# A mixer of attention and state-space heads in rounds of two jobs and two heads, with the weights' difference added while turned

## What is computed

```python
# attention branch: 8 heads, two score maps each, one subtracted from the other
a = probs(q1b, k1) - lam * probs(q2b, k2)
o = einsum('bhqk,bhkv->bhqv', a, v)            # then an RMS norm over each head's 64 columns
# state-space branch: 16 heads of 64 columns, in two groups of 8
y = einsum over keys of (C B^T * decay) with x*dt   # written over the whole 256 x 256 causal map
y = (y + xs * d_skip) * silu(z)                # then an RMS norm over each group's 512 columns
mixed = concatenate([attn, ssm]) @ w_out
```

## Times and the profile before

| | us |
|---|---|
| timed runs | 1287.53, 1287.18, 3872.66 (median 1287.53) |
| the profiled execution | 1286.62 |
| its span, first to last instruction | 1284.8 |
| mean granted clock of TensorE | 0.982 |

### The profile page before, as it was taken

How to read it: one execution, slowest core, us unless ns; L and a number is a source line. 1 busy time by engine, 2 the same in 40 slices (tenths; PEclk the granted TensorE clock), 3 DMA queues, 4 the chain that set the end, 5 groups by cost and what they waited for, 6 DMA issues and landing times.

```text
span 1284.8 us, 19110 instructions
## 1 busy us (share of the span) xinstructions
PE 1223.2 (95%) x7700; PEld 1058.4 (82%) x7700; DVE 839.2 (65%) x1308; ACT 656.0 (51%) x1076; POOL 230.9 (18%) x284
## 2 busy tenths in 40 slices
PE   7897899999999889999999999999999889999996
PEld 6785588888888568888888889999996579888996
DVE  6955586665586467666657776467766756766743
ACT  6425566644333556664446555446635444655531
POOL 4003431110000332121112221000005201112101
PEclk9999999999999999999999999999999879999999
DMA  7790155564454324555544554543440024455461
GB/s 275 269 200 14 54 197 171 190 222 174 163 197 155 141 99 173 188 196 194 184 182 162 196 198 153 197 175 141 162 185 1 1 77 162 164 196 175 155 206 56
DMA packets 34088, 205.56 MB, mean 160 GB/s; under 512 B 3776, under 2 KB 6352, under 8 KB 13776
## 3 DMA queue, kind: packets, MB, share of 16 engines
q1 hardware_dynamic: 30704, 200.47, 44.0%
q10 hardware_dynamic: 3296, 3.87, 1.6%
HBM read 202.87 MB, written 1.46 MB: 159 GB/s over the span
## 4 chain that ended last, share of the span: by engine, by line
PE 79%; DVE 14%; ACT 3%; POOL 1%; issue 1%; DMA 0%; POOLq 0%; ACTq 0%; DVEq 0%
PE ps L660 35%; PE ps L665 23%; PE ps L663 5%; PE ps L664 5%; DVE wl L602 4%; PE ps L684 1%; PE ps L686 1%; PE ps L685 1%; DVE tf L2173 1%; POOL pb L992 1%; PE ps L907 1%; PE ps L973 1%; ACT wh L573 1%; DVE y L1960 1%; DVE xb L738 1%
## 5 line engine op out<-in xcount | busy, mean ns | idle before, releaser
L602 DVE TENSOR_TENSOR wl<-raw,wh 128x2048 fp32r<-128x2048 f32 (+4 forms) x196 | 421.2, 2154 | 150.6 <-ACT wh L573 150.4
L660 PE MATMUL ps<-xb,wh 128*128 128x512 f32 x1424 | 502.3, 398 | 4.4 <-DVE wl L602 3.9
L665 PE MATMUL ps<-xb,wl 128*128 128x256 f32 x1696 | 476.2, 281 | 0.0
L573 ACT ACTIVATE wh<-raw 128x2048 fp32r<-128x2048 f32 (+4 forms) x196 | 348.6, 1781 | 157.9 <-PE ps L665 123.6
L660 PEld LDWEIGHTS ps<-xb,wh 128*128 128x128 f32 x1424 | 267.4, 188 | 71.1 <-issue 5.6
L665 PEld LDWEIGHTS ps<-xb,wl 128*128 128x128 f32 x1696 | 321.5, 190 | 0.0
L665 PE MATMUL ps<-ab,wl 128*128 128x256 f32 x1088 | 307.2, 282 | 0.0
L660 PE MATMUL ps<-ab,wh 128*128 128x512 f32 x640 | 226.8, 399 | 0.8 <-DVE ab L1002 0.8
L665 PEld LDWEIGHTS ps<-ab,wl 128*128 128x128 f32 x1088 | 207.0, 190 | 0.0
L660 PEld LDWEIGHTS ps<-ab,wh 128*128 128x128 f32 x640 | 120.2, 188 | 31.7 <-DVE ab L1002 1.4
L857 DVE TENSOR_TENSOR tf<-ps,tf 128x256 f32<-128x256 f32 x148 | 61.9, 421 | 119.3 <-ACT tf L852 119.3
(11 more groups left out here) (326 smaller groups left out, 1372.1 us busy)
## 6 DMA issues: line engine op xcount, KB each, us to landing
raw<-wstream SPq DMA_DIRECT2D x156, 1024.0 KB, 4.8
raw<-wstream SPq DMA_DIRECT2D x32, 704.0 KB, 4.1
raw<-wstream SPq DMA_DIRECT2D x8, 768.0 KB, 4.2
e_bt<-scratch ACTq DMA_DIRECT2D x16, 128.0 KB, 9.7
o_bt<-scratch SPq DMA_DIRECT2D x2, 1024.0 KB, 10.2
raw<-wstream SPq DMA_DIRECT2D x2, 560.0 KB, 10.1
raw<-wstream SPq DMA_DIRECT2D x4, 256.0 KB, 6.4
h<-xt ACTq DMA_DIRECT2D x4, 256.0 KB, 7.5
```

Of the source, the lines that this page charges most:

```text
L573: e.g.activation(WH[i % HLN][:, 0:w], RAW[i % RAWN][:, 0:w], ACT.Copy).then_inc(S["hi"], 1)
L602: e.g.tensor_tensor(WL[q][:, 0:w], RAW[i % RAWN][:, 0:w], f32(WH[q][:, 0:w]), ALU.subtract).then_inc(S["lo"], 1)
L660: e.g.matmul(PS[b][:, :].rearrange("p (a t) -> p a t", a=2), wh[:, sl], x2[:, :, cs], start=start, stop=k == p.nk - 1, skip_group_check=pair)
L665: ins = e.g.matmul(o, wl[:, sl], xh[:, cs], start=False, stop=k == p.nk - 1, skip_group_check=pair)
```

## The change

The mixer's loop goes from 30 steps to 13 rounds, and a round takes one attention head (two jobs) and two state-space heads. The map of decays is laid out so that its first two blocks have one bias.
- **PE.** `pe_decay(p)` builds heads 2p and 2p+1 in banks 3 and 4. The fp32 product for the first block is gone; the split of dt*a into two fp32r parts (SPL, now for both token blocks) is multiplied with two 256-column stretches of trir: four fp32r products of 256 columns and two masks. `pe_states(p)` does the products of the two heads interleaved, `pe_mixer_scores(h)` the scores of the head's two jobs interleaved (banks 7 and 2), `pe_mixer_pv(s)` the value products of two heads interleaved. `pe_mixer_turn(h)` does six accumulating products with the identity as the moving operand, for each block the first job's weights and then the second's, instead of three transposes of a sum. A round is: group sum, scores(i), turn(i-1), decay(i+2), states(i+1), in odd rounds a value pair, attention sum.
- **ACT.** Two exponentials for a state-space head, not three. Its round is: exponentials of two jobs, copy of turn(i-1), `act_decay(i+2)`, m_oa in odd rounds, late steps.
- **POOL.** Weights one of the two state-space heads (`weighted`), squares for the attention norm, multiplies y by silu(z), squares and sums it, and weighs both jobs (`pool_weigh`).
- **DVE.** Maxima of two jobs, weights the other state-space head, adds d_skip*x, late steps, then both reciprocals, the second times -lambda.
- **Before the loop.** Decays 0 and 1 and the xt and cb products stand ahead of mv, states(0) behind it. m_eb has four buffers; m_xdt and m_eb lie elsewhere, so some of the ah copies wait for the last state product. `MIXK` puts state-space tiles first.
- **The even attention.** ACT takes jobs 2 and 3's exponentials before ev1's outputs; DVE computes the gates of one token block in step 7 and of the other in step 9; the compressed branch's transposes move from step 6 to step 11.

The core of the diff:

```diff
-MIXK = [0, 1, 2, 4, 5, 6, 7, 8, 9, 10, 11, 3]
+MIXK = [4, 5, 0, 6, 7, 1, 8, 9, 2, 10, 11, 3]
...
+        def pe_mixer_turn(e, h):
+            A = MIX
+            j = A.pv_base + h
+            b = A.TB[0]
+            e.wait_ge(S["wt"], A.base + 2 * h + 2)
...
+            for x in range(3):
+                s = slice(x * 128, x * 128 + 128)
+                e.g.matmul(PS[b][:, s], PB[2 * h % 4][:, s], c_("ident"), start=True, stop=False)
+                ins = e.g.matmul(PS[b][:, s], PB[(2 * h + 1) % 4][:, s], c_("ident"), start=False, stop=True)
+            ins.then_inc(S["tp"], 1)
...
# pe_mixer
+            pe_decay(e, 1)
+            pe_toks(e, G["mv"], x_ready(5))
+            pe_states(e, 0)
+            for i in range(ROUNDS):
+                for kind, s, step in late_steps(i):
+                    if (kind, step) == ("grp", 1):
+                        e.wait_ge(S["gq"], 4 * s + 4)
+                        pe_sums(e, "ones512", (ACC, ACC2)[s][:, :], nb_no(kind, s))
+                if i < 8:
+                    pe_mixer_scores(e, i)
+                if 0 <= i - 1 < 8:
+                    pe_mixer_turn(e, i - 1)
+                if i + 2 < 8:
+                    pe_decay(e, i + 2)
+                if i + 1 < 8:
+                    pe_states(e, i + 1)
+                if i % 2 and 0 <= i - 3 < 8:
+                    pe_mixer_pv(e, (i - 3) // 2)
+                for kind, s, step in late_steps(i):
+                    if (kind, step) == ("sub", 2):
+                        e.wait_ge(S["sbq"], s + 1)
+                        pe_sums(e, "head64", TMP[0][:, 0:T], nb_no(kind, s))
...
# pool_mixer
+            for i in range(ROUNDS):
+                if i + 1 < 8:
+                    weighted(i + 1)
                 for kind, s, step in late_steps(i):
                     if kind == "sub" and step == 1:
                         e.wait_ge(S["oa"], s + 1)
...
+                if i < 8:
+                    acc, y = (ACC, ACC2)[i // 4][:, :], Y[:, tile(i)]
+                    e.wait_ge(S["yd"], i + 1)
+                    e.wait_ge(S["zs"], 4)
+                    e.link(e.g.tensor_tensor(y, y, m_zs[:, tile(i)], ALU.mult))
...
+                    for j in (2 * i, 2 * i + 1):
+                        pool_weigh(e, A, j, A.base + j)
...
# dve_mixer
+            for i in range(ROUNDS):
+                for j in (2 * i, 2 * i + 1):
+                    if j < A.n:
+                        dve_max(e, A, j)
+                if i + 1 < 8:
+                    weighted(i + 1)
+                if i < 8:
+                    y = Y[:, tile(i)]
+                    e.wait_ge(S["sy"], i + 1)
...
                 for kind, s, step in late_steps(i):
...
+                for j in (2 * i, 2 * i + 1):
+                    if j < A.n:
+                        e.wait_ge(S["ex"], A.base + j + 1)
+                        r = rs(j)
+                        if j % 2 == 0:
+                            e.g.reciprocal(r, sm(j)).then_inc(S["iv"], 1)
...
         def late_steps(i):
-            return ([("sub", s, i - 4 * s - 6) for s in range(4) if 1 <= i - 4 * s - 6 <= 4]
-                    + [("grp", g, i - 7 * g - 7) for g in range(2) if 1 <= i - 7 * g - 7 <= 6])
+            return ([("grp", g, i - 4 * g - 3) for g in range(2) if 1 <= i - 4 * g - 3 <= 4]
+                    + [("sub", s, i - 2 * s - 2) for s in range(4) if 1 <= i - 2 * s - 2 <= 4])
...
# the even attention
                 if i == 2:
+                    act_exp_biased(e, A, 2)
+                    act_exp_biased(e, A, 3)
                     act_gemm(e, G["ev1"], drain=act_toks(G["ev1"], e_v, 512, 0), ahead=0)
...
-                if i == 4:
-                    dve_even_gates(e)
+                if i in (7, 9):
+                    dve_even_gates(e, i // 9)
```

More of the change, by code:

```diff
@@ new lines, in pe_decay @@
+        def pe_decay(e, p):
+            e.wait_ge(S["spl"], 1)
+            for x in range(2):
+                h, ps = 2 * p + x, PS[DB[x]]
+                if p == 0:
+                    e.wait(G["mixer"].free.get(DB[x]))
+                else:
+                    e.wait_ge(S["sx"], h - 2 + 1)
+                for part in range(2):
+                    e.g.matmul(ps[:, 0:256], SPL[:, 32 * part + h:32 * part + h + 1].broadcast_to([128, 128]),
+                               trir[:, 128:384], start=part == 0, stop=False, skip_group_check=True)
+                for part in range(2):
+                    a = 32 * part + 16 + h
+                    e.g.matmul(ps[:, 128:384], SPL[:, a:a + 1].broadcast_to([128, 128]), trir[:, 0:256], start=False,
+                               stop=False, skip_group_check=True)
+                e.g.matmul(ps[:, 0:128], identb[:, :], maskkb[:, :], start=False, stop=False, skip_group_check=True)
+                e.g.matmul(ps[:, 256:384], identb[:, :], maskkb[:, :], start=False, stop=True,
+                           skip_group_check=True).then_inc(S["sd"], 1)
@@ new lines, in pe_states @@
+        def pe_states(e, p):
+            if p == 0:
+                e.wait(G["mixer"].free.get(YB))
+                e.wait(G["xt3"].out[0])
+            else:
+                e.wait_ge(S["yd"], p)
+            e.wait_ge(S["smu"], p + 1)
+            e.wait_ge(S["smv"], p + 1)
+            o = [PS[YB][64 * x:64 * x + 64, :] for x in range(2)]
+            vs = [slice(64 * (2 * p + x), 64 * (2 * p + x) + 64) for x in range(2)]
+            for x in range(2):
+                e.g.matmul(o[x][:, 0:256], m_xdt[0][:, vs[x]], eb(p, x)[:, 0:256], start=True, stop=False)
+            for x in range(2):
+                ins = e.g.matmul(o[x][:, 128:256], m_xdt[1][:, vs[x]], eb(p, x)[:, 256:384], start=False, stop=True)
+            ins.then_inc(S["sy"], 1)
@@ L2418, in pe_mixer_scores @@
+        def pe_mixer_scores(e, h):
+            A = MIX
+            ps = [PS[b] for b in A.SB]
+            t0, sl = (h // 2) * T, slopeb[:, h * 128:h * 128 + 128]
+            p_ = [slice(64 * (h % 2) + 32 * x, 64 * (h % 2) + 32 * x + 32) for x in range(2)]
+            if h == 0:
+                e.wait(G["mixer"].free.get(2))
+                e.wait_ge(S["na"], 1)
                 e.wait(G["mk"].out[1])
             else:
-                e.wait_ge(S["ex"], A.base + i - 2 + 1)
-            e.g.matmul(ps[:, 0:128], m_q[p_, t0:t0 + 128], m_k[p_, t0:t0 + 128], start=True, stop=False)
@@ new lines, in pe_mixer_turn @@
+        def pe_mixer_turn(e, h):
+            A = MIX
+            j = A.pv_base + h
+            b = A.TB[0]
+            e.wait_ge(S["wt"], A.base + 2 * h + 2)
+            if h:
+                e.wait(turned(j - 1))
+            else:
+                e.wait(G["mixer"].free.get(b))
+            for x in range(3):
[3 more added lines that the diff above has]
+            ins.then_inc(S["tp"], 1)
@@ new lines, in pe_mixer_pv @@
+        def pe_mixer_pv(e, s):
+            A = MIX
+            if s == 0:
+                e.wait(G["mixer"].free.get(OB))
+                e.wait(G["mv"].out[1])
+            else:
+                e.wait_ge(S["oa"], s)
+            hs = (2 * s, 2 * s + 1)
+            for h in hs:
+                e.wait(turned(A.pv_base + h))
+            for h in hs:
+                e.g.matmul(PS[OB][64 * (h % 2):64 * (h % 2) + 64, 0:256], m_v[0][:, 64 * h:64 * h + 64],
+                           PT[(A.pv_base + h) % 3][:, 0:256], start=True, stop=False)
+            for h in hs:
+                e.g.matmul(PS[OB][64 * (h % 2):64 * (h % 2) + 64, 128:256], m_v[1][:, 64 * h:64 * h + 64],
+                           PT[(A.pv_base + h) % 3][:, 256:384], start=False, stop=True).then_inc(S["pv"], 1)
```

373 lines of the change are left out of this document (144 added, 229 removed).

## The result

The kernel after takes 1283.2 us in the median of 7 runs (1278.65 to 1284.39), the kernel before 1287.85 in the same comparison: a ratio of 0.9952, 95% interval 0.9933 to 0.997. A second comparison, of 12 runs against 21, gave 0.9961 (0.9945 to 0.9977). So the change makes the kernel 0.4 to 0.5% faster, 5 us, where 1290, 2.5 us slower, was forecast. The time lies inside the forecast range, but the forecast had the wrong sign.

The account below looks back on a forecast made before the run. TensorE, busy 95% of the span, was taken as the bound, with other engines binding in parts of the mixer. 1284.8 + 4.6 (mixer) - 2.0 (first attention) = 1287.4 span, 1290.1 median; forecast 1284 to 1296, eight in ten 1278 to 1301.

Parts of the forecast that it names:

- The order of the waits: Mixer loop: in-order POOL and VectorE queues idle TensorE, 3.5 us before scores(4), 4.2 before turn 5.
- The tail: Mixer's end: ScalarE's roots and VectorE's norms free mo's first bank 8.5 us after turn 7.
- the walk's length at full clock: Mixer loop followed wait by wait at full clock: mo starts at 1039.8, against 1040.2 before.
- the entry: Loop's start: decay 0 waits 0.6 us for VectorE's split; loop begins at 967.4, scores(0) end at 969.0.
- the weighing ends 6.7 after its scores: Rounds 0 to 3: 1.2 for maxima, 0.54, 0.5, POOL's 2.3 and 2.05, and waits, before the turn.
- The clock term: Mixer: TensorE work at 1.2 GHz after idle costs 5 us, bounds 0 and 8.3; mo starts at 1044.8.
- First attention: Exponentials of jobs 2 and 3 run under ev1's product; turn 3 comes 2.5 earlier; gain 2.0 us, bounds 0 and 4.5.
- The step from span to median: Whole kernel: the timed runs' median lies 2.7 us above the profiled span, taking 1287.4 to 1290.1.
- The waits overlap more: Rival, mixer: a third of the 26 us idle doesn't come, mo starts at 1036, time 1281; chance 0.24.
- VectorE and POOL keep each other out: Rival, mixer: VectorE operations slowed beside POOL's, 0.3 us lost on each, mo 10 later, time 1300; chance 0.20.
- The turning stays cheap: Rival, mixer turns: an identity product costs as a transpose, 8 us of work go, time 1286; chance 0.03.
- 8 us of saved TensorE work turn into idle time: Mixer loop: TensorE's work falls from 58 to 50 us, but waits leave mo at 1039.8 against 1040.2.

Follow-up runs that it names:

- fill: Kernel after plus 118 small products, results never read, in TensorE's five idle places of the mixer; 1274.6 us, ratio 0.9878.
- turn_half: Kernel after without the second product of each pair in a turn, so the second job's weights are not added; 1280.5 us, ratio 0.992.
- dve_weighted: Kernel after with POOL's product of decays and C.B given to VectorE, which then does both of a round; 1282.7 us, ratio 0.996.
- mixer_only: Kernel after with the first attention's edits taken back, leaving the new mixer; 1289.2 us, ratio 0.9997.
- best3: Kernel after with POOL's square behind the weighings, VectorE's reciprocals ahead of its late steps, and the last sum's bank read earlier; 1267.9 us, ratio 0.983.

## Why the prediction was wrong
**The order of the waits was right.** Idle ahead of round 4's sum, released by POOL's sum: forecast 3.5, measured 3.38. Ahead of turn 5, by POOL's weighing: 4.2 and 4.61. The 5 walked between value pair 2 and turn 7 came as 3.47 ahead of the sum of round 8 and 1.20 ahead of turn 7; which place the 3 stood for the walk does not say. The experiments show the cause that was named: with the square moved the stalls ahead of both group sums vanish. The tail from the last turn's end to mo, 8.5 forecast, was 7.8.

**The failed step is the walk's length at full clock, in "The order".** It put mo at 1039.8, 92.0 us into the mixer (947.82 is its start before), and said "if the clock holds at 1.00 in the loop, mo starts near 1040". `fill` holds the clock, and mo starts 86.0 us in. Against the forecast's milestones (us into the mixer):

| | forecast, full clock | fill | after |
|---|---|---|---|
| scores(0) end | 21.2 | 20.2 | 20.2 |
| turn 0 starts | 27.9 | 25.6 | 25.6 |
| turn 2 starts | 40.0 | 36.9 | 37.0 |
| value pair 0 ends | 44.6 | 41.2 | 41.3 |
| turn 4 starts | 58.0 | 53.2 | 56.2 |
| turn 5 starts | 68.4 | 63.8 | 66.8 |
| turn 6 starts | 74.2 | 69.1 | 74.4 |
| turn 7 ends | 83.5 | 78.2 | 85.1 |
| mo starts | 92.0 | 86.0 | 92.9 |

1.0 us goes at the entry and 2.4 more by the end of value pair 0. The term there was "the weighing ends 6.7 after its scores": turn 0 starts 5.4 after them. POOL in round 0 of the kernel after shows both parts of the 1.3:
```profile
966.36 0.73 POOL L2152 TENSOR_TENSOR y<-y,m_zs 128x256 f32<-128x256 f32 x1 [14.21 <-DVE y L2260]
...
967.17 0.61 POOL L2155 TENSOR_TENSOR acc<-y 128x256 f32<-128x256 f32 x1
...
967.76 1.63 POOL L965 TENSOR_SCALAR pb<-pb,rs 128x128 f32<-128x128 f32 x4
```
A weighing takes 1.63 and not 2.05, and the first head of a group has nothing to add its square to, so that 1.4 us stand ahead of the weighing where 2.3 were walked. In the later rounds the shorter weighing stays. This loop, not TensorE's work, sets rounds 0 to 3 (`turn_half`). Decays at 0.65 for 0.83 and score pairs at 1.42 for 1.6 add up to 16x0.18 + 8x0.18 = 4.3 us less work, less 0.4 for the state pairs, but only part of it is on the path. Another 1.7 us go by the end of value pair 1 (62.6 against 57.5), 1.3 of them between scores(4) and turn 4, walked at 7.8 and measured at 6.5 in `fill`; 0.9 go behind it.

**The clock term was under, not over.** 5 us were taken of 0 to 8.3; the new mixer pays 6.9. The two errors, -6.0 and +1.9, give 92.9 in place of 97.0: the mixer is 0.5 us longer than in the profile of before, not 4.6.

**What the clock term was held against was missed altogether.** The sum went against one execution of the kernel before, whose mixer had 27 us of low clock, and whose clock of 0.982 is above the kernel's mean of 0.979. Other executions have 34 and 41. The new rounds always have 27. So the mixer part is neutral against the execution that was read, and the median of before was not that execution's.

**First attention.** The mechanism was right (the exponentials of jobs 2 and 3 run under ev1, turn 3 comes 2.9 earlier by the two profiles; 2.5 was forecast), its size was 2.7 to 3.3 us at equal clock where 2.0 was taken of 0 to 4.5. The half microsecond set down for the moved gates isn't seen in this size, and the bound's clause, no low clock after it, is partly what happened: 2.0 us of it between 100 and 160 in the mean, 7.4 before.

**The step from span to median.** The forecast span was 1287.4, the measured one 1282.6: 4.8 over, 4.1 from the mixer and 0.8 from the first attention (between the two and behind mo, -1.2 and +1.2 against before cancel). The 2.7 us from span to median were before's; after's median lies 0.6 above its profiled span. That adds 2.1 and makes 6.9, 1290.1 against 1283.2.

**The rivals.** "The waits overlap more" (1281) is the one that came near, but not by its mechanism: the stalls came in full. "VectorE and POOL keep each other out" (mo 10 us later) did not come: at full clock mo starts 6 us ahead of the walk, and `dve_weighted` gains nothing by taking POOL's products away. "The turning stays cheap" fell with 1.36 us a turn; `turn_half` shows that half of the turning is worth 4.7 us of the mixer, all of it from round 4 on. The reason given against a gain, that 8 us of saved TensorE work turn into idle time, held: `mixer_only` gains nothing.

## To carry to other kernels
In an in-order queue, put what waits for a late result behind what others wait for: one 0.6 us square moved behind the weighings was worth 9 us; the reciprocals behind it brought nothing that could be told when moved alone, and were worth some 4 once the square was out of the way. Idle time of TensorE costs a second time where gap-free TensorE work follows at the low clock, and nothing more where other engines' chains follow; small products in the gaps tell the two apart. And read a kernel's profile more than once before you hold a sum of a few microseconds against it: two executions of one program differed here by 14 us of low clock in one stage.

## What the runs showed of the hardware
- The granted clock after the same stalls is not the same in each execution: in the kernel before's mixer 27, 41 and 34 us at 1.2 GHz. In the new rounds it was 27 in all six profiles.
- A microsecond at 1.2 GHz costs 0.34 us of span over the 21 executions of before, nothing in `best3`'s mixer, and half where TensorE has no gaps (67 and 83 products in mo's first 10 us, with 4 and 0 us of low clock).
- From some 90 to 98 us TensorE runs at 1.2 GHz for 3 to 7 us in 17 of the 18 profiles (the clock is 0.62 to 0.81 from 88 to 96), although it is busy for 7.5 to 8.0 of these 8 us. In `mixer_only`'s first profile it is as busy (7.51) and the clock stays at 1.00; what follows stands 2.3 us earlier there (the first turn at 100.18, in before at 102.53).
- Two jobs' scores on 32 rows each, interleaved, cost 1.42 us, 0.09 more than one job's 1.33; the products of the second job are nearly free. The Trainium skill (TensorE: Matmul & The Clock Gate, Part 3: Packing small matmuls — row/col tiling) says that tiles in different row groups run at once; the trace agrees with these 0.09.
- A VectorE product of two SBUF operands takes 0.80 us in the mean beside POOL's and 0.575 without. The Trainium skill (SBUF — State Buffer, 🔬 SBUF: two separate sides) says that the shared pair of ports is locked for a whole instruction; the trace agrees in that VectorE's product takes up to 1.06 us beside POOL's, and `dve_weighted`'s time shows no gain without it.
